# Experts with at most 64 rows in plain fp32 on two halves of the array, and gate and up weights in 8 KB pieces

## The reference

```
def hier_moe(h, w_rg, b_rg, w_re, b_re, w_ei, w_eo):
    ...
    g = jnp.argmax(lg, axis=-1)
    ...
    top_v, top_i = lax.top_k(le_g, TOP_K)                    # TOP_K = 2
    eid = (g[:, None] * EXPERTS_PER_GROUP + top_i).reshape(-1)
    ...
    gu = lax.ragged_dot(xs, w_ei, sizes)                     # w_ei: 32 x 2048 x 1024
    gate, up = jnp.split(gu, 2, axis=-1)
    ys = lax.ragged_dot(jax.nn.silu(gate) * up, w_eo, sizes) # w_eo: 32 x 512 x 2048
    y = jnp.zeros_like(hf).at[tok_s].add(ys * w_s[:, None].astype(ys.dtype))
```

## Time and profile before

| | us |
|---|---|
| median of 3 runs (3588.44 to 3592.2) | 3590.94 |
| the profiled execution | 3590.53 |
| its span, from the first to the last instruction | 3588.5 |
| the loop over the experts, first product to last (about 2105 to 3496) | 1390 |
| TensorE busy / DVE / ACT / POOL | 3366.8 / 1683.9 / 1288.3 / 1021.6 |

### The profile page before, as it was taken

How to read it: one execution, slowest core, us unless ns; L and a number is a source line. 1 busy time by engine, 2 the same in 40 slices (tenths; PEclk the granted TensorE clock), 3 DMA queues, 4 the chain that set the end, 5 groups by cost and what they waited for, 6 DMA issues and landing times. The chain is left out here.

```text
span 3588.5 us, 51245 instructions
## 1 busy us (share of the span) xinstructions
PE 3366.8 (94%) x18439; PEld 2950.7 (82%) x18440; DVE 1683.9 (47%) x1742; ACT 1288.3 (36%) x1577; POOL 1021.6 (28%) x761
## 2 busy tenths in 40 slices
PE   8999999999999998989999869999999999999990
PEld 8999999999999975668888657787888788778770
DVE  4222222000111147860111267658888858846677
ACT  4000000000000035750101246657787757746572
POOL 3444444444444301234445431101111101101010
PEclk9999999999999998999999879999999999999995
DMA  4121111212222391116445469679999979967688
GB/s 150 60 67 54 54 54 58 76 61 75 87 80 67 124 348 61 54 42 238 156 124 164 152 216 356 244 258 354 364 353 369 360 253 369 370 218 268 255 336 361
DMA packets 341083, 691.62 MB, mean 193 GB/s; under 512 B 23034, under 2 KB 151482, under 8 KB 330511
## 3 DMA queue, kind: packets, MB, share of 16 engines
q1 hardware_dynamic: 291508, 585.75, 45.9%
q10 hardware_dynamic: 37163, 66.14, 4.9%
q0 software_dynamic: 12336, 38.69, 3.1%
HBM read 637.25 MB, written 97.28 MB: 205 GB/s over the span
## 5 line engine op out<-in xcount | busy, mean ns | idle before, releaser
L1979 DVE TENSOR_TENSOR e_w_lo<-expert_raw,e_w_hi 128x2048 fp32r<-128x2048 f32 x388 | 872.8, 2288 | 255.1 <-ACT e_w_hi L1891 231.9
L1891 ACT ACTIVATE e_w_hi<-expert_raw 128x2048 fp32r<-128x2048 f32 x388 | 744.3, 1919 | 301.9 <-PE e_gu L1805 253.3
L295 PE MATMUL p_z<-hT_hi,p_w_hi 128*128 128x384 f32 x2256 | 755.3, 335 | 2.4 <-DVE p_xs L432 2.4
L297 PE MATMUL p_z<-hT_hi,p_w_lo 128*128 128x384 f32 x2256 | 753.8, 334 | 0.0
L296 PE MATMUL p_z<-hT_lo,p_w_hi 128*128 128x384 f32 x2256 | 753.7, 334 | 0.0
L295 PEld LDWEIGHTS p_z<-hT_hi,p_w_hi 128*128 128x128 f32 x2256 | 423.6, 188 | 2.7 <-DVE p_xs L432 2.7
L296 PEld LDWEIGHTS p_z<-hT_lo,p_w_hi 128*128 128x128 f32 x2256 | 423.6, 188 | 0.0
L297 PEld LDWEIGHTS p_z<-hT_hi,p_w_lo 128*128 128x128 f32 x2256 | 423.5, 188 | 0.0
L1805 PE MATMUL e_gu<-e_w_hi,e_xT_hi 128*128 128x512 f32 x1216 | 390.4, 392 | 6.6 <-issue 6.6
L1805 PE MATMUL e_gu<-e_w_lo,e_xT_hi 128*128 128x512 f32 x1216 | 387.8, 390 | 0.0
L1805 PE MATMUL e_gu<-e_w_hi,e_xT_lo 128*128 128x512 f32 x1216 | 387.8, 390 | 0.0
(11 more groups left out here) (337 smaller groups left out, 4642.4 us busy)
## 6 DMA issues: line engine op xcount, KB each, us to landing
expert_raw<-w_ei SPq DMA_DIRECT2D x256, 1024.0 KB, 8.6
expert_raw<-w_eo SPq DMA_DIRECT2D x128, 1024.0 KB, 10.4
p_w_raw<-w_in SPq DMA_DIRECT2D x96, 512.0 KB, 4.0
m_w_raw<-w_out SPq DMA_DIRECT2D x64, 512.0 KB, 4.4
d_k<-cache_k SPq DMA_DIRECT2D x8, 2048.0 KB, 14.6
d_v<-cache_v SPq DMA_DIRECT2D x8, 2048.0 KB, 9.9
rows_back<-expert_rows SPq DMA_DIRECT2D x12, 1024.0 KB, 15.8
n_x<-x SPq DMA_DIRECT2D x9, 1024.0 KB, 5.9
```

The costliest lines, as they stand in the source:

```text
L295: pe.matmul(out, w_hi[:, k, :], x_hi[:, xk, cols], start=(k == 0), stop=False)
L297: mm = pe.matmul(out, w_lo[:, k, :], x_hi[:, xk, cols], start=False, stop=(k == KT - 1))
L1891: act.activation(w_hi[:, s, :], raw[:, r, :], ACT.Copy).then_inc(hi_done, 1)
L1979: dve.tensor_tensor(w_lo[:, s, :], raw[:, r, :], w_hi[:, s, :], ALU.subtract).then_inc(lo_done[r], 1)
```

## The change

It does six things.

1. A table `group_kind` gives each group a kind: small (at most 64 rows; never the first group), full (65 to 128) or pair. `by_kind` chooses among three bodies on TensorE, ACT, DVE and POOL. TensorE and ACT run through all 40 passes without a test against the count.
2. A small group's units are not split. TensorE multiplies the raw fp32 weights by the fp32 rows: for each block of 128 rows two products of 64 rows (`up_small`), one into partitions 0 to 63, one into 64 to 127 of one bank; the output likewise, two units side by side (`out_small`). So silu and product are one instruction each on 128 partitions, and the output half rows are stored in pieces of 4 KB by a second set of row numbers, `twice`.
3. DVE keeps an exact copy `xT` of the first 64 turned rows for every group.
4. The second tile of a pair is turned at the start of the pair itself, and the first four units' products run for the first tile before they run for the second.
5. A unit of gate and up is two neighbouring rows for each partition, 8 KB in one piece; the rows of the tokens are turned by every second column to match (`columns_of`). The output's units come in the order 0, 2, 1, 3.
6. Rows are gathered for both tiles of every group. The place rows have six fields instead of four, and are cleared by three transfers instead of one.

The core of the diff:

```diff
-        w = c.io.w_ei.rearrange("e (u a p) n -> e u p a n", a=2, p=P)[...]
+        w = c.io.w_ei.rearrange("e (u p a) n -> e u p a n", a=2, p=P)[...]
...
+        def columns_of(r, k):
+            return x[:, r, :].rearrange("p (u q a) -> p u a q", a=2, q=P)[:, k // 2, k % 2, :]
...
-                    gather_tile(0)
-                    with pool.If(before < after):
-                        gather_tile(1)
+                    for r in range(2):
+                        gather_tile(r)
...
+                    def up_small():
+                        pe.wait_ge(x_kept, 4 * (g + here + 1))
+                        pe.wait_ge(x_exact, 4 * (g + 1))
+                        pe.wait_ge(a_kept, 2 * (g + here) + 1)
+                        bank = gu_ps[:, 0, :].rearrange("p (b n) -> p b n", b=2)
+                        for u in range(UIN):
+                            pe.wait_ge(raw_loaded[u % RAW], 32 * g + 16 * (u // RAW) + 16)
+                            for a in range(2):
+                                k = 2 * u + a
+                                w = raw[:, u % RAW, a * 1024:(a + 1) * 1024].rearrange("p (b h n) -> p b h n", b=2, h=2)
+                                for h in range(2):
+                                    mm = pe.matmul(bank[side(h)], xT[:, k, :], w[:, :, h, :], start=(k == 0), stop=(k == KT - 1))
...
+                            mm.then_inc(lo_done[u % RAW], 1)
...
+                    def out_small(i):
+                        units = [UIN + 2 * i + h for h in range(2)]
+                        for u in units:
+                            pe.wait_ge(raw_loaded[u % RAW], 32 * g + 16 * (u // RAW) + 16)
...
+                        for k in range(KE):
+                            for h, u in enumerate(units):
+                                mm = pe.matmul(y_ps[side(h), i, :], aT[:, k % 2, side(k // 2)], raw[:, u % RAW, k * 512:(k + 1) * 512],
+                                               start=(k == 0), stop=(k == KE - 1))
...
+                    def group(kind):
+                        if kind == SMALL:
+                            up_small()
+                            pe.wait_ge(x_loaded, 32 * (g + 2))
+                            turn_rows(g + 1, g + here + 1, 0, (0,))
+                            turn_act_small()
+                            turn_rows(g + 1, g + here + 1, 0, (1, 2, 3))
+                            for i in range(UOUT // 2):
+                                out_small(i)
+                        else:
+                            up_and_first(tiles_of(kind))
+                            out_rest(tiles_of(kind))
...
                 def keep_rows_lo(tile, r, quads):
                     for q in quads:
                         dve.wait_ge(x_hi, 4 * tile + q + 1)
+                        dve.tensor_copy(xT[:, 4 * q:4 * q + 4, :], bank(t_ps, q % 2)[:, :, 0:FEW]).then_inc(x_exact, 1)
                         dve.tensor_tensor(quad(xT_lo, r, q), bank(t_ps, q % 2), quad(xT_hi, r, q), ALU.subtract).then_inc(x_kept, 1)
```

More of the change, by code:

```diff
@@ L1570, in groups, with all_groups, kind_of, by_kind @@
                     body(g)
+        def all_groups(eng, body):
+            with eng.Fori(0, MAXG) as g:
+                body(g)
         def pairs(eng, g):
             return eng.value_load(c.group_pairs[0:1, ds(g, 1)], min_val=0, max_val=MAXG)
[L1576 to L1581, removed]
+        def kind_of(eng, g):
+            return eng.value_load(c.group_kind[0:1, ds(g, 1)], min_val=0, max_val=PAIR)
+        def by_kind(eng, g, part):
+            kind = kind_of(eng, g)
+            for k in (SMALL, FULL, PAIR):
+                with eng.If(kind == k):
+                    part(k)
+        def tiles_of(k):
+            return 2 if k == PAIR else 1
+        def column_twice(g, f):
+            return twice[:, ds(g, 1), f:f + 1].rearrange("p a b -> p (a b)").bitcast(F32)
         def field(g, f):
@@ L1641, in gather_tile, with gather @@
                         ap=gather_idx[:, r:r + 1].bitcast(U32), axis=0), bounds_check=TOK - 1, oob_is_err=False).then_inc(x_loaded, 16)
-                def gather(g, before, after):
+                def gather(g):
                     c.hold(pool)
@@ L1679, in _ @@
                 count = group_count(pool)
-                p0, p1, p2 = (pairs(pool, g) for g in range(3))
+                p1 = pairs(pool, 1)
                 pool.wait_ge(x_cleared, 2)
@@ L1683, in _ @@
                 c.hold(pool)
-                gather_tile(0)
-                with pool.If(p0 < p1):
-                    gather_tile(1)
+                for r in range(2):
+                    gather_tile(r)
                 for n in range(LEAD, NP):
@@ L1754, in _ @@
                 pe.wait_ge(plan_ready, 1)
[L1755 to L1760, removed]
+                pe.wait_ge(x_loaded, 32)
+                turn_rows(0, 0, 0, range(4))
                 def body(g):
-                    here, nx, nx2 = (pairs(pe, g + i) for i in range(3))
+                    here = pairs(pe, g)
                     def turn_act(r, h):
@@ L1812, in up_and_first @@
                             pe.wait_ge(lo_done[u % RAW], 2 * g + u // RAW + 2)
-                            if u < UIN - 1:
+                            if n == 2 and u < SPL:
+                                for a in range(2):
+                                    for x_part, w_part in PASSES:
+                                        for h in range(2):
+                                            mm = product(u, a, 1, x_part, w_part, h)
+                            elif u < UIN - 1:
                                 for a in range(2):
@@ L1945, in activate, with keep @@
                         keep_rows_hi(g + here + n, 0, (2, 3))
-                    by_size(act, here, nx, activate)
-                    with act.If(nx < nx2):
-                        for q in range(4):
-                            act.wait_ge(x_turned, 4 * (g + nx + 2) + q + 1)
-                            act.activation(quad(xT_hi, 1, q), second_bank(q).rearrange("p (a b) -> p a b", a=4), ACT.Copy).then_inc(x_hi, 1)
-                    split_hi(g, UN - 1)
-                    act.wait_ge(y_free, g + 1)
-                    c.hold(act)
-                    def keep(n):
+                    def keep(n, split):
                         for b in range(UOUT):
@@ L1972, in _, with keep_small @@
-                groups(act, count, body)
+                            if split:
+                                split_hi(g + 1, b)
+                    def keep_small(split):
+                        for i in range(UOUT // 2):
+                            if split:
+                                split_hi(g + 1, i)
+                            for h in range(2):
+                                product_done(UIN + 2 * i + h)
+                            c.hold(act)
+                            act.activation(y[:, 0, i * 512:(i + 1) * 512], y_ps[:, i, :], ACT.Copy,
+                                           scale=column_twice(g, 0)).then_inc(y_kept, 2)
+                        for u in range(UOUT // 2, UOUT if split else 0):
+                            split_hi(g + 1, u)
```

249 lines of the change are left out of this document (178 added, 71 removed).

## The result

The changed kernel takes 3543.0 us (median of four runs, 3536.9 to 3547.0), the kernel before 3591.6 beside it: ratio 0.9864, interval 0.9845 to 0.9882. So it is faster, as forecast, but by 48.5 us instead of 115. The profiled execution took 3536.9 us, its span is 3535.2 against 3588.5 before: 53.3 less.

The account below looks back on a forecast made before the run. TensorE was taken as the bound (busy 94%), with DMA engines already 95% busy in full experts. Small experts -133, transitions +10, copies +18, moved turns -20, start +5, clock +5: -115 from 3590.5, about 3475 us, range 3430 to 3545.

Parts of the forecast that it names:

- doubled turns: Turns reading every second column in bigger experts: taken as free, at worst twice as long, 40 us in all.
- 30 for copies: Exact copies on DVE delaying the last splits in bigger experts: upper end 30 us, +18 us taken.
- six units are already loaded: Small expert behind a bigger one: half its loads already there, TensorE sets 26 against 35.8 us, 78 us gained over eight.
- +10 for all transitions: Small to bigger expert, eight times: TensorE waits 0.5 us six times and 3.4 us twice for the first unit.
- TensorE's waits for late splits in full experts: Listed among the signs, in the profile after, that would show the forecast wrong; no size given.
- by about 20: Small expert behind a bigger one: its other six units land by about 20 us, before the output products want them.
- The long run: Nine small experts, third or later in a row: set by loads at 31.5 instead of 35.8 us, 39 us gained.
- Rival 1: Long run gains nothing, as buffers come free in bursts and loads fall behind: 3514 us, chance 0.14.
- TensorE's own time: Small expert on TensorE: 24 fp32 product pairs at 0.86 us plus 5.0 us between, 25.7 us.
- Rival 2: Small experts' array halves run one after another, 1.72 us a pair: slower, 3808 us, chance 0.06.
- Rival 3: TensorE's loop with a third body stalls on code, some 5 us an expert: 3605 us, chance 0.05.
- moved turns of the second tile: Second tile turned at the pair's own start, hidden behind first-tile products: -20 us over six pairs.

Follow-up runs that it names:

- experiment 7: The kernel before, with only the 8 KB pieces and the turns of every second column, no small kind: 3591.2 us, ratio 0.9999.
- Experiments 2: The changed kernel, with the four lone small experts ahead of a full one done as full ones: 3541.6 us, ratio 0.9861.
- experiment 3: The changed kernel, with every load after the first six bringing half of its unit, products still in full on old data: 3427.5 us, ratio 0.9545.
- experiment 4: The changed kernel, with the two lone small experts ahead of a pair done as full ones: 3549.5 us, ratio 0.9881.
- experiment 1: The changed kernel, with each load of output weights halved for every expert, products still in full on old data: 3496.0 us, ratio 0.9727.
- experiment 11: The changed kernel, with DVE's two table waits behind the four subtractions for the next expert instead of ahead: 3539.6 us, ratio 0.9863.
- experiment 10: The changed kernel, with the small kind's bound set to 0, so every one-tile expert is done as full: 3595.8 us, ratio 1.0017.

## Why the prediction was right in sign and wrong in size

The time lies inside the forecast's own range of 3430 to 3545, by 2 us, and that is luck: the upper end was made of doubled turns (40), which cost nothing in experiment 7, and of 30 for copies, which cost 0.4 in a full expert.

The account by parts, first product to first product of the next expert, forecast and measured (us, after minus before):

| part | forecast | measured |
|---|---|---|
| 4 lone small ahead of a full expert, with that full one | -32.5 | +1.6 |
| 2 lone small ahead of a pair, with that pair | -23.8 | -12.6 |
| first small of each of two runs | -19.6 | -15.0 |
| second of each run, one with the pair behind it | -14.8 | -5.8 |
| 8 inside the long run | -34.4 | -23.7 |
| the last of the run, with the pair behind it | -3.5 | -1.7 |
| other bigger experts | 0 | -4.4 |
| the start (first two experts) and the end | +9 | +8.1 |
| the clock | +5 | in the rows above |
| sum | -115 | -53.5 |

**The step that failed: "six units are already loaded".** The forecast counted the full buffers as a gift to each small expert behind a bigger one: 9.8 us times 8. They are a loan. At the end of every full expert the buffers are full, before the change and after, so between two such points the DMA engines must bring 24 units whatever TensorE does. The prediction had itself read that a steady full expert fills them 95%; by that row two experts in 72 us leave 5%, 3.5 us, to gain, not 9.8, and over the two shown above even less. It charged the small expert's wait into the next one at 0.5 us (+10 for all transitions), where the four full experts wait 2.1 to 3.2 at their first product, because it asked when the next unit lands, and not what becomes of the four units that ACT and DVE otherwise split in advance. Its own sign for that, TensorE's waits for late splits in full experts, is there: 13.1 of the 14.4 us, in 7 of the 9 waits; 7.9 us of waits for the activation come on top. Experiments 2 and 3 show both halves: without the small expert ahead, the full one takes 36.3; with half the bytes, 37.4 behind a small one. This is 34 of the 61 us that went missing.

**Ahead of a pair** the loan is free, as experiment 4 shows, but the gain is 5 us, not 9.8, in the undisturbed one: TensorE waits 1.8 us for the eighth unit and 0.8 for the output's second pair, since the loads begin only when its first units are used, 2.1 us after its start. The forecast had the last landed "by about 20". With half the loads (experiment 3) this expert takes 29.6 us instead of 33.0. Of the 11 us that are missing in this row of the table, 4.4 are the wait without a releaser in the other one. The best case, the 9th expert, behind a full one and ahead of a small one, took 27.5 us where 26 was forecast, and with the 10th 60.7 where 53 was forecast: in the first 57 us the queue of the weights moved 21.0 MB, twenty loads and not eighteen, since those for the expert behind were under way too.

**The long run.** That the small experts in it are set by loads was right, at 32.9 instead of 31.5 us. The mis-sized term is the rate: 396 GB/s measured in the stretch itself, where 434 had been taken from the last stage and 389 and 406 from windows of 3 us. Twelve loads of 1.05 MB and 0.49 MB of rows an expert are 13.1 MB, at 396 GB/s 33.0 us. The last small expert of the run takes 37.2 us without the gap in which the pair's turns lie; the gather of the pair's 205 rows, issued 6 us ahead of its start, comes before its loads, and TensorE waits for two of them 2.1 and 2.9 us. Rival 1 (the run stays at 35.8) fell, but its mechanism is there: with shorter output loads in experiment 1 the run came to 31.0 instead of 27.5. There TensorE waits for loads while the DMA engines are busy 0.91 of the nine periods, which fits buffers that come free in bursts.

The Trainium skill, "DMA: Bandwidth & Descriptors", section "Where 436 GB/s comes from", bounds loads from HBM at about 358 GB/s. By that rule an estimate for 13.1 MB is 36.6 us, and the run would have gained nothing. The trace disagrees: 396 GB/s over 296 us, 406 with 8 KB pieces throughout.

**TensorE's own time.** Right: two records of 0.43 us side by side, 0.86 us a pair. In the timeline of the run a unit's two pairs (eight records) end 1.94 us after their start with the tail of the last in it, and then TensorE waits for the next load:

```profile
2514.96 1.94 PE L1941 MATMUL e_gu<-expert_raw,e_xT 128*64 128x512 f32 x8 [0.54 <-DMA expert_raw<-w_ei]
2517.47 1.94 PE L1941 MATMUL e_gu<-expert_raw,e_xT 128*64 128x512 f32 x8 [0.57 <-DMA expert_raw<-w_ei]
```

25.9 us at full clock in experiment 3, against 25.7 forecast. Rival 2 fell.

**Code.** Rival 3, a fetch at every expert, fell: the list of queues for 2230 to 3450 us again has no instruction queue.

```profile
q1 hardware_dynamic: 94697, 365.13, 77.3%
q0 software_dynamic: 13824, 33.08, 7.2%
```

But most kernels stand once or twice in their first experts for 4 to 8 us without a releaser (4.4 after, 7.7 in experiment 11, 5.9 in 10, 6.6 before), and from 2085 to 2230 us the queue moved 7 blocks, where before it moved 4 up to 2160 and none from there on the earlier trace rows. That these are first fetches of the new bodies fits, but no run took the fetch away; it stays an inference.

**The rest.** Copies: 0.4 us in an undisturbed full expert, not 2.0; DVE had the room. The moved turns of the second tile gave some 15 us in experiment 10 (the five experts ahead of a pair 10.3, the pair ahead of a pair 5.3), 20 forecast. The start cost 7.4 where 9 was forecast with its two copies, by causes that no run separates: the waits without a releaser and the slow loads beside the tables, below, both lie there. The prediction also left out the wait on DVE, since it names no work queued behind the two table waits, and there were four subtractions; but experiment 11 gained nothing by moving it. The end moved by 0.7.

## What to carry to other kernels

Work that is hidden behind one expert's surplus has to be budgeted from one full-buffer point to the next: add up the bytes of all the stages between the two points and divide by the rate of that very stretch, and only then credit a stage that became shorter. A stage that saves engine time but not bytes gains where its neighbour leaves the DMA engines idle, and nothing where they were 95% busy. Where loads set the time, look at the smallest pieces first: here the 2 KB pieces of the output were worth more than the 4 KB ones that the change had enlarged.

## What the hardware showed that was not expected

**Loads beside tables of 16-byte elements go at half the rate.** At the start POOL reads the table of places in 16-byte elements, now with `twice` beside it. Its landing took 23.9 us, 13.8 before (the DMA issues of 2105 to 2165 us: count, KB each, us from issue to landing; first after, then before), and in that time the DMA engines were full at 215 GB/s (a window of after, third fence):

```profile
e_table<-slots POOLq DMA_DIRECT2D x1, 160.0 KB, 23.9
```

```profile
e_table<-slots POOLq DMA_DIRECT2D x1, 160.0 KB, 13.8
```

```profile
2122.00:2146.00 24.00, 21.53 (x100) 16.88 (x98) 15.23 (x17) 18.26 (x19) 4.77 (x3) 1.00 1.01 215
```

The Trainium skill, "DMA: Bandwidth & Descriptors", section "Why small descriptors are slow (HBM only)", says that each DMA operation carries a fixed cost beside its bytes. The trace agrees in direction: beside 246 KB of tables the full engines moved 215 GB/s for 24 us, about half of the 396 of the long run. In the other runs with `twice` and whole loads the table took 18.8 to 24.6 us, in experiment 7, without `twice`, 14.2, and in experiment 3, with half the loads, 11.2. No run here took the tables away, so that they alone halve the rate is not shown.

**The clock in a small expert.** In the changed kernel TensorE was busy 3.65 of 5.5 us in one activation of the long run, and the output products behind it began at a granted clock of 0.51, the lower of the two levels (1.2 GHz):

```profile
2519.30:2524.80 5.50, 3.65 (x20) 2.59 (x18) 3.07 (x7) 2.25 (x4) 0.00 (x0) 0.85 1.05 388
2524.80:2526.60 1.80, 1.80 (x7) 0.55 (x8) 1.73 (x4) 0.60 (x1) 0.58 (x2) 0.51 1.08 420
```

With half the loads (experiment 3) TensorE waits for no load in the run. It has a mean clock of 0.94 there, and eight of its nine periods are 27.3 us, where four small experts at 1.00 take 25.9 to 26.8: about 1 us each. The output products alone last 8.2 us in one of the run and 7.1 in a lone one at 1.00. In the changed kernel the run is set by the loads, so there most of that should be hidden.
